# Attention's k, q, v and out projections as three products of rounded halves, with ten transfers through five buffers

## What is computed

```
k, v = split(modulate(rms_norm(h, kv_norm_g), shift, scale) @ kv_w, 2)
k = rms_norm(k.reshape(b, s, 16, 64), k_norm_g)
q = rms_norm((hn @ w_q).reshape(b, s, 16, 64), q_norm_g)
sc = einsum("bqhd,bkhd->bhqk", qc, kc) * scale + bias
p = softmax(where(valid, sc, -1e30));  out = einsum("bhqk,bkhd->bqhd", p, vc)
h = h + g1 * (out @ w_o)
```

## Time and profile before

| | us |
|---|---|
| median of 3 runs | 1988.56 (1987.9 to 1991.34) |
| the profiled execution | 1990.02 |
| its span, first to last instruction | 1987.3 |
| PE busy | 1910.5 (96%) |
| DVE busy | 675.4 (34%) |
| ACT busy | 590.7 (30%) |
| attention, from the last x of the MLP (1621.62) to the last square (1787.06) | 165.4 |

### The profile page before, as it was taken

One profiled execution on the slowest core, in us unless ns is written; L12 is line 12 of the kernel. 1 busy time (PEld: TensorE's weight loads), 2 busy tenths in 40 slices (PEclk: granted clock), 3 DMA queues, 4 the chain that ended last, 5 costly groups with the idle time before them and its releaser, 6 DMA issues.

```text
span 1987.3 us, 27614 instructions
## 1 busy us (share of the span) xinstructions
PE 1910.5 (96%) x11543; PEld 1321.5 (66%) x11543; DVE 675.4 (34%) x1189; ACT 590.7 (30%) x988; POOL 66.7 (3%) x136
## 2 busy tenths in 40 slices
PE   5999999979999999999999999999999999999998
PEld 2888685323334888685333335766699988588998
DVE  4583413000003583413000003304355551426554
ACT  2325311111113325311111112042244532535443
POOL 0000001101001000001101001000000000000000
PEclk9999999989999999999999999999999999999999
DMA  9669753999976665753999957779954453233540
GB/s 390 265 258 385 296 245 140 427 428 428 427 307 232 258 254 222 297 246 145 428 427 427 407 196 291 316 313 429 398 206 176 169 211 111 80 128 139 198 170 21
DMA packets 52734, 541.09 MB, mean 272 GB/s; under 512 B 6816, under 2 KB 11168, under 8 KB 21664
## 3 DMA queue, kind: packets, MB, share of 16 engines
q1 hardware_dynamic: 42656, 505.66, 63.1%
q0 software_dynamic: 9984, 34.09, 4.6%
HBM read 589.53 MB, written 29.62 MB: 312 GB/s over the span
## 4 chain that ended last, share of the span: by engine, by line
PE 81%; DMA 8%; DVE 6%; ACT 2%; DVEq 1%; issue 1%; SPq 0%; POOL 0%; POOLq 0%; ACTq 0%
PE bank L940 15%; PE bank L1242 14%; PE bank L903 9%; PE bank L904 9%; PE bank L905 9%; PE bank L1266 7%; DMA ring<-in_w_up 5%; PE bank L950 3%; PE bank L1068 2%; PE bank L1448 1%; PE bank L1356 1%; DMA ring<-in_ada 1%; PE bank L1377 1%; DMA ring<-in_lru_w_out 1%; DVE h_t L2106 1%
## 5 line engine op out<-in xcount | busy, mean ns | idle before, releaser
L903 PE MATMUL bank<-split_x,split_w 128*128 128x256 f32 x1024 | 290.0, 283 | 2.4 <-DVE split_w L2423 2.4
L904 PE MATMUL bank<-split_x,split_w 128*128 128x256 f32 x1024 | 289.8, 283 | 0.0
L905 PE MATMUL bank<-split_x,split_w 128*128 128x256 f32 x1024 | 289.8, 283 | 0.0
L903 PEld LDWEIGHTS bank<-split_x,split_w 128*128 128x128 f32 x1024 | 196.6, 192 | 3.4 <-DVE split_w L2423 3.4
L2305 DVE TENSOR_TENSOR hidden<-cqkv,bank 128x256 f32<-128x256 f32 x46 | 19.4, 421 | 522.2 <-ACT cqkv L1703 522.2
L904 PEld LDWEIGHTS bank<-split_x,split_w 128*128 128x128 f32 x1024 | 196.6, 192 | 0.0
L905 PEld LDWEIGHTS bank<-split_x,split_w 128*128 128x128 f32 x1024 | 196.6, 192 | 0.0
L2423 DVE TENSOR_TENSOR split_w<-ring,split_w 128x1024 fp32r<-128x1024 f32 x128 | 156.3, 1225 | 92.8 <-ACT split_w L1816 92.8
L940 PE MATMUL bank<-h_t,ring 128*128 128x256 f32 x736 | 161.9, 380 | 6.3 <-DVE h_t L2278 3.1
L1816 ACT ACTIVATE split_w<-ring 128x1024 fp32r<-128x1024 f32 x128 | 133.8, 1050 | 92.4 <-PE bank L905 91.4
L940 PEld LDWEIGHTS bank<-h_t,ring 128*128 128x128 f32 x736 | 139.1, 190 | 30.0 <-DVE h_t L2106 4.0
(11 more groups left out here) (355 smaller groups left out, 2418.1 us busy)
## 6 DMA issues: line engine op xcount, KB each, us to landing
ring<-in_ada SPq DMA_DIRECT2D x48, 2048.0 KB, 11.8
ring<-in_w_down SPq DMA_DIRECT2D x32, 2048.0 KB, 16.0
ring<-in_w_gate SPq DMA_DIRECT2D x32, 2048.0 KB, 12.4
ring<-in_w_up SPq DMA_DIRECT2D x32, 2048.0 KB, 17.5
ring<-in_mlp_w SPq DMA_DIRECT2D x32, 2048.0 KB, 7.8
ring<-in_w_in SPq DMA_DIRECT2D x16, 2048.0 KB, 11.7
mix<-in_w_gate SPq DMA_DIRECT2D x14, 2048.0 KB, 15.0
mix<-in_w_up SPq DMA_DIRECT2D x14, 2048.0 KB, 19.5
```

The costliest lines, as they stand in the source:

```text
L903: pe.matmul(out, hi, x_hi, start=start, stop=False, **kw)
L904: pe.matmul(out, hi, x_lo, start=False, stop=False, **kw)
L905: return pe.matmul(out, lo, x_hi, start=False, stop=stop, **kw)
```

## The change

What it does, piece by piece.

**Products.** Each tile of k, q and out (`split_tile`) is 24 products of fp32r halves in place of 8 float32 ones, and each v job 24 in place of 8. The weight matrices are cut into 32 parts of 128 columns. ACT rounds a part into one of four places in slot 5 (`a_hi`), DVE writes the rest over the part in its slot (`a_part`). Part n may be rounded once the job that used part n-4 is done: `A_PARTS` names that job, and for parts 20 to 23 it is v1, for 24 to 27 v3. The inputs of k and v, of q, and of out are rounded in two halves each (`round_half`, `rest_of_half`).

**Waits.** PE no longer waits for transfers; ACT does, at a part's first use. The tile of part 0, 8 or 24 waits for the halves of x as they come; every other tile waits for DVE's rest of its part; `values` waits for all four rests of its parts. The wait for B ov3 ahead of out0 is gone, since the half of o is waited for.

**Transfers.** Slots 0 to 4 in the order of use: k, k, q, q, v, v, bias a, bias b, out, out. The sixth goes into slot 0 after k1, the bias tables into slots 1 and 2 after k3 and q1, the out weights into slots 3 and 4 after q3 and v1. `p2_[1]` moves to slot 0, and the MLP after it starts in slots 1, 2, 0 and 3, the last of these after out1.

```diff
+A_PARTS = ([f"k{i // 2}" for i in range(8)] + [f"q{i // 2}" for i in range(8)] + ["v1"] * 4 + ["v3"] * 4
+           + [f"out{i // 2}" for i in range(8)])
...
+A_SLOT = [0, 1, 2, 3, 4, 0, 1, 2, 3, 4]
...
+A_LAST = ["k1", "k3", "q1", "q3", "v1", "v3", None, None, "out1", "out3"]
+A_SOURCE = [0, 1, 2, 3, 4, 5, 8, 9]
...
-MLP_SLOTS = [[0, 1, 2, 3], [2, 3, 0, 1]]
+MLP_SLOTS = [[0, 1, 2, 3], [1, 2, 0, 3]]
...
+        def a_hi(n):
+
+            at = (SLOTS - 1) * SLOT + PART * (n % PARTS)
+            return ring_lo[:, at:at + PART].rearrange("p (k c) -> p k c", k=KT)
...
+                if n % 8:
+                    pe.wait_ge(VA.sem, VA.at(f"part{n}"))
+                    for i, k in places_:
+                        one(hi, x_hi, i, k, first=(i + k == 0))
+                        one(hi, x_lo, i, k)
+                        ins = one(lo, x_hi, i, k, last=(i + k == 4))
+                    return ins
+                for halves_ in ([(0,), (1,)] if by_half_of_x else [(0, 1)]):
+                    for i in halves_:
+                        pe.wait_ge(AA.sem, AA.at(f"{x} half{i}"))
+                        pe.wait_ge(AA.sem, AA.at(f"part{n}"))
+                        for k in range(4):
+                            one(hi, x_hi, i, k, first=(i + k == 0))
+                    pe.wait_ge(VA.sem, VA.at(f"part{n}"))
+                    for i in halves_:
+                        for k in range(4):
+                            one(lo, x_hi, i, k)
+                    for i in halves_:
+                        pe.wait_ge(VA.sem, VA.at(f"{x} half{i}"))
+                        for k in range(4):
+                            ins = one(hi, x_lo, i, k, last=(i == 1 and k == 3))
...
+                    for j in range(n, n + 4):
+                        pe.wait_ge(VA.sem, VA.at(f"part{j}"))
...
+                        pe.matmul(out, x_hi, hi[:, k], start=(k == 0), stop=False)
+                        pe.matmul(out, x_lo, hi[:, k], start=False, stop=False)
+                        ins = pe.matmul(out, x_hi, lo[:, k], start=False, stop=(k == KT - 1))
...
-            pe.wait_ge(AA.sem, AA.at("B ov3"))
...
+                if n < PARTS:
+                    act.wait_ge(MLP[0][0].sem, MLP[0][0].at("part7", MLP_TURNS - 1))
+                else:
+                    act.wait_ge(PA.sem, PA.at(A_PARTS[n - PARTS]))
+                act.activation(a_hi(n), a_part(n, ring), ACT.Copy).then_inc(AA.sem, AA.one(f"part{n}"))
...
             values(0)
             values(1)
+            round_a_parts(20, 24)
             head_norm("qn", mix[:, 11264:13312])
             values(2)
             values(3)
+            round_a_parts(24, 28)
...
+            round_half("o", 0)
             for g in range(6):
                 transposed_act(nc, act, a_of, PA, AA, 0, "B ", g, pT2)
             outputs_act(nc, act, a_of, PA, AA, 0, "B ", o2_[:, 4:8, :])
...
+            round_half("o", 1)
+            round_a_parts(28, 30)
...
+                    tt(a_part(n, ring_lo), a_part(n, ring), as_f32(a_hi(n)), ALU.subtract)\
+                        .then_inc(VA.sem, VA.one(f"part{n}"))
...
+            rest_of_a_parts(24, 28)
...
+            rest_of_half("o", 0)
             for g in range(6):
                 normed_dve(nc, dve, AA, VA, 0, "B ", g, p2_[1], sums[1])
-            into_x(VA, PA, a_bank, mod[:, 2 * KT:3 * KT])
+            rest_of_half("o", 1)
+            rest_of_a_parts(28, 30)
```

More of the change, by code:

```diff
@@ L465 @@
           + [(f"out{i}", "dve") for i in range(4)] + [("norm2", "act")])
[L466 to L471, removed]
@@ L472, with a_parts, halves_of @@
-A_UNITS = [("kv_w_2", P, KT, 0, 512 * i, 512) for i in range(4)]
+A_PARTS = ([f"k{i // 2}" for i in range(8)] + [f"q{i // 2}" for i in range(8)] + ["v1"] * 4 + ["v3"] * 4
+           + [f"out{i // 2}" for i in range(8)])
+def a_parts(first, end):
+    return [f"part{n}" for n in range(first, end)]
+def halves_of(name):
+    return [f"{name} half{i}" for i in range(2)]
+A_ACT = SQ0 + a_parts(0, 1) + ["norm"] + a_parts(1, 2) + halves_of("k") + a_parts(2, 4)
+A_ACT += ["k0"] + a_parts(4, 6) + ["k1"] + a_parts(6, 8) + halves_of("q") + ["k2"] + a_parts(8, 10) + ["k3"]
@@ L473 @@
+A_DVE += a_parts(8, 16) + ["k"] + a_parts(16, 20) + ["bias"] + a_parts(20, 24) + ["q"] + a_parts(24, 28)
+A_DVE += six("A s") + both(six("A p"), six("B s")) + ["o half0"] + six("B p") + ["o half1"] + a_parts(28, 30)
+A_DVE += ["out0"] + a_parts(30, 32) + ["out1", "out2", "out3"] + H2 + ["h lo0", "h lo1", "x"]
+A_UNITS = [("kv_w_2", P, KT, 0, 512 * i, 512) for i in range(2)]
 A_UNITS += [("attn_w_q_2", P, KT, 0, 512 * i, 512) for i in range(2)]
+A_UNITS += [("kv_w_2", P, KT, 0, 512 * i, 512) for i in range(2, 4)]
@@ L1419, in _, with split_tile, one @@
             keep_busy(pe, banks[7], 15)
-            pe.wait_ge(VA.sem, VA.at("h 0"))
-            def projected(name, u0, rhs, which=range(4)):
+            def split_tile(out, n, x, by_half_of_x=False):
+                hi, lo = a_hi(n), a_part(n, ring_lo)
+                x_hi, x_lo, _ = a_x[x]
+                places_ = [(i, k) for i in range(2) for k in range(4)]
+                def one(a, b, i, k, first=False, last=False):
+                    return pe.matmul(out, a[:, 4 * i + k, :], b[i][:, k, :], start=first, stop=last)
+                if n % 8:
[19 more added lines that the diff above has]
+                            ins = one(hi, x_lo, i, k, last=(i == 1 and k == 3))
+                return ins
@@ L1849, in _ @@
                 taken(f"k{i}", k2_[:, 2 * i:2 * i + 2, :])
+                round_a_parts(4 + 2 * i, 6 + 2 * i)
+                if i == 1:
+                    act.wait_ge(VA.sem, VA.at("hq"))
+                    for half in range(2):
+                        round_half("q", half)
             act.drain()
@@ L1886, in _ @@
             outputs_act(nc, act, a_of, PA, AA, 0, "B ", o2_[:, 4:8, :])
-            norm_act(AA, VA, PA, a_bank, SQ2, "norm2", [VA.at(f"out{i}") for i in range(4)])
+            act.drain()
+            round_half("o", 1)
+            round_a_parts(28, 30)
+            for i in range(4):
+                act.wait_ge(VA.sem, VA.at(f"out{i}"))
+                act.activation(h_t[:, 2 * i:2 * i + 2, :], x_t[:, 2 * i:2 * i + 2, :], ACT.Square)\
+                    .then_inc(AA.sem, AA.one(SQ2[i]))
+                if i == 0:
+                    round_a_parts(30, 32)
+            act.wait_ge(PA.sem, PA.at("norm2"))
+            rstd(act, a_bank["norm2"], rs[:, 0, :], D).then_inc(AA.sem, AA.one("norm2"))
             round_stream(AA, VA)
@@ L2448, in _, with rest_of_a_parts, rest_of_half @@
             dve.drain()
+            def rest_of_a_parts(first, end):
+                for n in range(first, end):
+                    dve.wait_ge(AA.sem, AA.at(f"part{n}"))
+                    tt(a_part(n, ring_lo), a_part(n, ring), as_f32(a_hi(n)), ALU.subtract)\
+                        .then_inc(VA.sem, VA.one(f"part{n}"))
+            def rest_of_half(x, i):
+                hi, lo, raw = a_x[x]
+                dve.wait_ge(AA.sem, AA.at(f"{x} half{i}"))
+                tt(lo[i], raw[i], as_f32(hi[i]), ALU.subtract).then_inc(VA.sem, VA.one(f"{x} half{i}"))
+            rest_of_a_parts(0, 1)
             dve.wait_ge(AA.sem, AA.at("norm"))
             modulated(x_t, akv, modn[:, MODS:MODS + KT], rs[:, 0, :], VA, ["h 0", "h 1"])
+            for i in range(2):
+                rest_of_half("k", i)
+            rest_of_a_parts(1, 4)
             tt(hq, x_t, heads(rs[:, 0, :], KT), ALU.mult)
+            rest_of_a_parts(4, 6)
             dve.drain()
```

126 lines of the change are left out of this document (90 added, 36 removed).

## The result

The changed kernel takes 1997.16 us in the median of 6 runs (1996.26 to 2000.55), against 1988.80 us of the kernel before (6 runs, 1986.91 to 1991.34). The ratio is 1.0044, 95% interval 1.0032 to 1.0055: the medians are 8.4 us apart. The forecast was 1998.7 us. The ratios here are given as measured, with their intervals; the quotient of two medians can differ from them by some hundredths of a per cent.

A forecast was written before the change was run, and what follows sets the result against it. PE alone bounds the projections, DVE's unbroken row the scores and softmax. Products give -19.5 us; with waits and roundings attention is +5.1, with 5.0 of clock +10.1: 1998.7 us, range 1992 to 2003.

The forecast's parts named there:

- What the products give: Split products in k, q, out and v: 19.5 us won over 12 jobs and 4 v jobs, if nothing waits.
- ahead of v0: Between q3 and v0: PE waits 5.2 us for all four rests of parts 16 to 19.
- ahead of v2: Between v1 and v2: parts 20 to 23 wait for v1, so PE waits 3.5 us beside qn.
- the first score: Behind v3: rests 24 to 27 stand ahead in DVE's queue; 6.5 us after v3, a cost of 5.4 us.
- ahead of B pT0: Ahead of the B p transposes: PE idle 4.8 us, as B p0 waits for the first half of o.
- at the start: First k tile: PE idle 2.2 and 2.1 us for rounded halves and rests; 2.8 us lost.
- The clock: Granted clock falls behind the long waits: 5.0 us charged, at the start, v0 and v2, 0 at B p; 0 to 8.4 possible.
- The first half of o: Ahead of B p0: DVE waits for ACT's rounded half behind A ov's copy, then writes its rest; 6.9 us lost.
- the one in which the clock holds: Rival 1, attention: the waits come as worked out but the clock does not fall; +5.1 us, 1993.7 us, 15%.
- the one in which DVE's row is not what the softmax waits for: Rival 2, softmax: rests ahead of first score and B p cost nothing; 12.3 us fall away, 1980.6 us, 5%.
- The one of no change: Rival 3: wait for the half of o shorter by 3 us or more, one clock fall at most; 1985 to 1992, 9%.
- The one of four falls: Rival 4, worse: clock falls four times or stays low over v0 and v2, or a transfer is late; 2003 to 2010, 9%.

The follow-up runs named there:

- the last kernel: All repairs together against the changed kernel: v in pairs of parts, roundings and rests moved, 13 products of zeros at the start; 1971.48 us, ratio 0.9915 to the kernel before.
- the kernel with the filler: The changed kernel with PE's four long waits filled by products of zeros; 1992.2 us, ratio 1.0018 to the kernel before.
- the yardstick's execution: Profiled execution of the changed kernel run again with no edit; median 1998.9 us against 1988.9 of the kernel before, ratio 1.0047.
- their kernel: The kernel before with only the change's ten transfers, slots and SP waits, all products in float32; ratio 1.0005.
- moving the rests: The changed kernel with DVE's rests of parts 24 to 27 behind B p5, not ahead of the first score; 1993.7 us, ratio 1.0018 to the kernel before.
- Moving it: The changed kernel with DVE's rest of the first half of o behind B p5, not ahead of B p0; ratio 1.0017 to the kernel before.

## Why the prediction was right

**What the products give.** 1.15 us for a job of two tiles and 1.43 for a v job were forecast; the copies show 1.15 and 1.42. In the last kernel, where nearly nothing waits, this gain comes out. The estimate of about 27 us from the page "TensorE: Matmul & The Clock Gate" of the Trainium skill is refuted by the same rows: v jobs took 5.45 us, not 5.2.

**The waits.** All were at the places named and ended by the engines named. In size: 5.0 us ahead of v0 (forecast 5.2), 3.2 ahead of v2 (3.5), the first score 5.2 us later behind v3 (5.4), 4.4 ahead of B pT0 (4.8), 1.6 and 1.9 at the start (2.2 and 2.1). Each is 0.2 to 0.6 us under the forecast, and the waits cost 2.9 us over the products' gain and not 5.1, as the kernel with the filler shows. One term of all these waits on PE was misread: 0.55 us from the end of a rest to PE's first product. The 0.55 of the earlier trace rows is the time for which PE had been idle, and not the time since the rest ended. In DVE's timeline of the kernel before that rest ended at 71.65 + 2.36 = 74.01, and PE began at 74.16, 0.15 us later; at v0 of the kernel after it is 1682.90 + 2.36 = 1685.26 and 1685.54, 0.28 us:

```profile
71.65 2.36 DVE L2133 TENSOR_TENSOR ring_lo<-ring,ring_lo 128x1024 fp32r<-128x1024 f32 x2 [3.39 <-ACT ring_lo L1601]
```
```profile
1682.90 2.36 DVE L2581 TENSOR_TENSOR ring_lo<-ring,ring_lo 128x1024 fp32r<-128x1024 f32 x2 [3.39 <-ACT ring_lo L1914]
...
1685.54 0.77 PE L1523 MATMUL bank<-ring_lo,split_x 128*128 128x512 f32 x1 [4.99 <-DVE ring_lo L2581]
```

By place, the kernel with the filler against the forecast, the 2.2 us lie 0.5 at the start, 0.3 at v2, 0.2 at the first score, some 0.5 ahead of B p, 0.1 in q, and 0.6 in out: tile 24 was charged its whole gain for the wait for the second half of o, but from the copy of B ov3 to the last square it is 26.8 us against 31.4, which is the whole gain of eight tiles.

**The clock.** Forecast 5.0 us, as 1.7 at the start, 2.5 at v0, 0.9 at v2 and 0 at B pT; measured 6.9 us, as 2.4, 1.7, 1.7 and 1.1, and in the yardstick's execution 8.2 us, as 1.4, 2.8, 2.8 and 1.2. The charges at the first two places lie within what two executions of one kernel show; that of 0.9 at v2 was 0.8 to 1.9 us too low. The step that failed is the charge of 0 at B p: DVE paces the transposes only at full clock. At the lower one PE was the bound and had no gap, and it ended the last transpose 1.6 us after B p5, against 0.8 in the kernel with the filler. There were four falls, one at each of the four places of waiting. The Trainium skill ("TensorE: Matmul & The Clock Gate", "HAM oscillation") states that the cost of a fall is paid anew at each gap; the four falls in this trace agree with that.

**The sum.** Forecast +10.1 us; attention measured +9.8 in the profiled pair, and the medians +8.4. The two errors, 2.2 us too much for waits and 1.9 too little for the clock (by the first profile), cancel. So the forecast was right in its total by some luck, and in its mechanism by the experiments.

**The other steps.** The transfers at 0 are borne out by their kernel (ratio 1.0005, attention unchanged). The cost of the first score's delay was worked out as 5.4 us and moving the rests brings 5.2 from the copy of v3 to that of A ov3, and as much in the medians. The first half of o was worked out as 6.9 us; with the filler, so without the fall of the clock, it costs 6.4 from A ov3 to B ov3. Moving it brings 6.7 there (the 6.4 and the 1.1 of the fall, less 0.8 that ACT's rounding still costs), in the medians 5.9. Of the rivals, the one in which the clock holds is shown false for this kernel (its price of +5.1 would have been +2.9), and the one in which DVE's row is not what the softmax waits for falls with both moved rests: each brought more than 5 us. The one of no change falls with the ratio. The one of four falls came true in its condition and not in its price: the clock fell four times, but for 6.9 us in all and not the 8.4 that were counted as the most, behind shorter waits, and the time stayed under its 2003 us.

## What to carry to other kernels

Where a product is made cheaper by work on other engines, the gain must be counted against each place at which the new step stands ahead of something that is waited for: here 19.5 us of gain were eaten by steps at four places. At three of them it came back with no less work for any engine, by another place in the row or a finer unit (two parts in place of four); at the start 2.3 us stayed lost. DVE's work for a later stage went behind the chain of the present one, not where its buffer comes free. And the waits of PE here, 1.6 to 5 us long, cost more than themselves: products of zeros in them kept the clock and gave back 6.9 us in the profiled pair, 5.4 to 7.0 in the medians.

## What the runs showed of the hardware beyond what was expected

Two waits of 1.62 and 1.86 us with four products between them lowered the clock as one of 5 us did. In the first profile this fall had the largest price of the four, 2.4 us, but in four other executions with the same start it was 1.4 to 1.5 us. And behind one and the same wait the low clock lasted for different times in two executions of one kernel, with 12.3 and 13.3 us from the copy of q3 to that of v0. The price of a fall is therefore known here only to about 1 us. What decides how long the low clock lasts stays open.
